# A hybrid transformer stack in FP32: value projections by 512 columns, and five pieces of the engines' queues in another order

## The chip, the cores and the metric

The kernel runs on one core of one Trainium2 chip. The metric is the device time of one execution in microseconds (us), the median of several. TensorE (PE) multiplies, and its weight loads (PEld) run beside the multiplications; VectorE (DVE), ScalarE (ACT) and GpSimd (POOL) do the elementwise work; SyncE (SP) issues the DMAs. Each engine works through its own queue in order, and the queues meet at semaphores.

## The reference

Two blocks of two layers each run over 512 tokens of width 1024, all in FP32. Block one, per layer: feed-forward, a mixer (stick-breaking attention beside a gated delta rule), cross attention to a memory of 256 tokens, feed-forward. Block two, per layer: forgetting attention beside dilated attention (eight heads each), then a gated embedding. What the change touches:

```python
# block one, delta rule: its output is normed and gated before the output projection
go = gated_delta_rule(gq, gk, gv, g, beta)        # solves (lower + eye) per chunk of 64
go = rms_norm(go, gdn_out_norm) * silu(gdn_z)
# block one, memory: keys and values of 256 tokens, 1024 columns each
k, v = split(rms_norm(mem, mem_norm) @ w_kv, 2)
# block two: 512 tokens; values of 512 columns for each kind of head
z = rms_norm(h, norm_g) @ w_in                    # qa ka va ga fa qb kb vb gb
qa, ka, qb, kb = (rms_norm(heads) for each); qb, kb = partial_rope(qb), partial_rope(kb)
oa = forgetting_attention(qa, ka, va, log_f) * silu(ga)
ob = dilated_attention(qb, kb, vb) * silu(gb)
h = h + concat([oa, ob]) @ w_out
```

## The kernel before

**Slabs.** All weights lie in one stream of slabs, a slab being 128 partitions by 2048 numbers (1 MB): the 1024 rows of 256 columns of a weight matrix, as eight chunks of 128 rows. SP loads slab g into one of three buffers `slab_raw` as soon as slab g-3 is used up. ACT copies it, rounded, to `slab_hi` (two buffers, `high`, L313), and DVE writes the rest to `slab_lo` (`low`, L320). Each product of two FP32 matrices is three matmuls, hi·hi, hi·lo and lo·hi (`products`, L340), into PSUM banks.

**A projection stage** (`Project`) walks its slabs. On PE a slab of kind "pair" is 48 matmuls of 512 moving columns (the tokens), with the weights stationary. A slab of kind "tokens" (`tokens`) turns this round, since values are wanted with tokens on partitions: a block of 128 tokens is stationary and the slab's 256 columns move, so 96 matmuls of 256 columns for 512 tokens, 48 for the memory's 256. DVE's queue per slab: the stage's side work, the evacuation of the slab's banks, then `low` of the slab two further on. ACT's: side work, then `high` of the slab two further on. Four banks (0 to 3) take turns.

**Memory stage** (`cross_memory`): three slabs of keys (s = 0 to 2), four of values (s = 3 to 6), once per layer of block one. Its side work `GdnNorm` norms the delta rule's output: DVE scales (L2401, four operations) and multiplies with the gate (L2406, four) at s = 2, ACT rounds (L2377) at s = 3, DVE takes the rest (L2415) at s = 4.

**Delta rule's inverse** (`Mixer.vector`): the triangular inverse of 16 units (chunks 0 to 3 of four heads) is built by steps. For chunks 2 and 3 DVE prepares masks, units and transposes (`vector_first`, `vector_unit`, `vector_turn`), and PE's second product of the first step waits for the transpose of chunk 3. `vector_queries` (L2258) is an operation of DVE that this chain doesn't need.

**Block two's projection** has 15 slabs (4 query/key, 2 value, 2 gate slabs of the forgetting heads; 4, 2 and 1 of the dilated ones). Its side work `HeadNorm` norms the heads and turns the dilated ones (rope): PE rotates into banks 6 and 7, DVE multiplies with the sine (L1181, reads the banks) and the cosine (L1182) and adds (L1184).

**Attention stage** (`AttendPairs`), once per layer of block two: 24 units, three to each of eight head pairs. Per unit PE computes scores, DVE takes the row maximum (`top`, L2967), ACT the exponential (`exp`, L2923), DVE and POOL divide by the sum (`invert`, L2981; POOL L2900), PE transposes (`turn`, L2843), DVE and ACT copy out of PSUM (`keep`, L2988, L2932/L2933), PE multiplies with the values (`out`, L2860). The last gate slab is multiplied here too (`gate(0)`, `gate(1)`, 24 matmuls each, into banks 6 and 7), between the scores of the first units. POOL also writes the low half of the result of each head pair (`low`, L2910).

## Time and profile before

| | |
|---|---|
| median of 3 runs | 3196.43 us (3195.23 to 3198.82) |
| profiled execution | 3195.29 us, of which the span of the trace 3193.6 us |
| PE busy | 3146.7 us, 99% of the span, 17438 matmuls |
| PEld, DVE, ACT, POOL busy | 82%, 52%, 43%, 6% |
| mean DMA rate | 86 GB/s, 275 MB in all |

The span is the time from the first to the last instruction of the trace. Durations of matmuls overlap (the next begins before the last has ended), so the pace of PE is read from the starts of instructions. `[x <-engine tile line]` at a row's end is the time its engine stood idle ahead of it, and what ended that.

### The profile page before, as it was taken

To read this page: it belongs to the slowest core of one execution; us is meant where nothing else is said; L and a number is where in the kernel's file an instruction comes from. 1 tells how busy PE (TensorE), PEld (TensorE's weight loads), DVE (VectorE), ACT (ScalarE), POOL (GpSimd) and SP (SyncE) were. 2 spreads that over 40 slices of the span, in tenths; PEclk is the share of its full clock that TensorE was granted. 3 is DMA by queue.
4 is the path that set the end of the run, shared out by engine and by line. 5 is a ranking of instruction groups with operands and counts; after the bars stand their busy time and mean duration, and the time that the engine had idled before them with its cause. 6 is when DMAs were issued, how large, how long until landed. Compare 5 with 4: busy or idle time off the path is not lost.

```text
span 3193.6 us, 40800 instructions
## 1 busy us (share of the span) xinstructions
PE 3146.7 (99%) x17438; PEld 2612.5 (82%) x17438; DVE 1658.8 (52%) x2253; ACT 1363.0 (43%) x1759; POOL 188.3 (6%) x222
## 2 busy tenths in 40 slices
PE   9999999999999999999999999999999998999999
PEld 7888887898788888888887788788888886788777
DVE  5443348755544433443347855544433568554674
ACT  5222238554433223222226753432223557454663
POOL 0000001300000000000001300000000005000050
PEclk9999999999999999999999999999999999999999
DMA  4222221122122222222321112122222220122202
GB/s 178 94 88 94 109 72 61 41 106 93 66 92 100 86 100 101 102 93 86 112 80 67 54 67 107 66 92 93 102 89 103 80 93 28 71 104 83 80 29 85
DMA packets 47476, 275.13 MB, mean 86 GB/s; under 512 B 5312, under 2 KB 8896, under 8 KB 22208
## 3 DMA queue, kind: packets, MB, share of 16 engines
q1 hardware_dynamic: 47296, 272.53, 23.6%
q8 instruction: 138, 2.26, 0.3%
q14 instruction: 42, 0.34, 0.0%
HBM read 270.41 MB, written 2.10 MB: 85 GB/s over the span
## 4 chain that ended last, share of the span: by engine, by line
PE 90%; DVE 5%; ACT 3%; issue 1%; POOL 0%; DMA 0%; SPq 0%; DVEq 0%; ACTq 0%; POOLq 0%
PE banks L340 80%; PE banks L1617 1%; PE banks L2546 1%; PE banks L2587 1%; ACT slab_hi L313 1%; ACT weights L2923 1%; DVE weights L2967 1%; PE banks L1775 1%; PE banks L1653 1%; PE banks L1632 1%; PE banks L1252 0%; PE banks L1602 0%; DVE slab_lo L320 0%; DVE weights_turned L2988 0%; PE banks L1788 0%
## 5 line engine op out<-in xcount | busy, mean ns | idle before, releaser
L340 PE MATMUL banks<-x_hi,slab_hi 128*128 128x512 f32 x2560 | 1007.5, 394 | 9.6 <-DVE dil_qk L1182 7.9
L340 PE MATMUL banks<-x_hi,slab_lo 128*128 128x512 f32 x2560 | 998.2, 390 | 0.0
L340 PE MATMUL banks<-x_lo,slab_hi 128*128 128x512 f32 x2560 | 997.8, 390 | 0.0
L313 ACT ACTIVATE slab_hi<-slab_raw 128x2048 fp32r<-128x2048 f32 (+2 forms) x274 | 479.7, 1751 | 912.9 <-PE banks L340 912.9
L320 DVE TENSOR_TENSOR slab_lo<-slab_raw,slab_hi 128x2048 fp32r<-128x2048 f32 (+2 forms) x272 | 568.0, 2088 | 413.9 <-ACT slab_hi L313 413.9
L340 PEld LDWEIGHTS banks<-x_hi,slab_hi 128*128 128x128 f32 x2560 | 481.7, 188 | 116.2 <-issue 14.3
L340 PEld LDWEIGHTS banks<-x_lo,slab_hi 128*128 128x128 f32 x2560 | 481.9, 188 | 101.8 <-issue 2.9
L340 PEld LDWEIGHTS banks<-x_hi,slab_lo 128*128 128x128 f32 x2560 | 481.4, 188 | 101.2
L340 PE MATMUL banks<-hidden_hi,slab_hi 128*128 128x512 f32 x704 | 273.9, 389 | 0.0
L340 PE MATMUL banks<-hidden_lo,slab_hi 128*128 128x512 f32 x704 | 273.9, 389 | 0.0
L340 PE MATMUL banks<-hidden_hi,slab_lo 128*128 128x512 f32 x704 | 273.9, 389 | 0.0
L884 DVE TENSOR_TENSOR hidden<-banks,rstd 128x512 f32<-128x512 f32 x88 | 60.7, 690 | 311.1 <-PE banks L340 311.1
L861 DVE SCALAR_TENSOR_TENSOR h<-banks,h 128x512 f32<-128x512 f32 x80 | 55.2, 690 | 208.7 <-PE banks L340 208.6
L893 ACT ACTIVATE hidden_hi<-hidden 128x512 fp32r<-128x512 f32 x88 | 55.6, 632 | 252.9 <-DVE hidden L901 252.9
L340 PEld LDWEIGHTS banks<-hidden_lo,slab_hi 128*128 128x128 f32 x704 | 132.2, 188 | 27.6
L340 PEld LDWEIGHTS banks<-hidden_hi,slab_hi 128*128 128x128 f32 x704 | 132.2, 188 | 27.4
L340 PEld LDWEIGHTS banks<-hidden_hi,slab_lo 128*128 128x128 f32 x704 | 132.2, 188 | 27.3
L1224 POOL MEMSET token_w<- 128x1024 f32 x4 | 3.8, 954 | 2036.7 <-PE banks L340 2036.7
L340 PE MATMUL banks<-slab_hi,x_hi 128*128 128x256 f32 x384 | 109.0, 284 | 0.0
L340 PE MATMUL banks<-slab_hi,x_lo 128*128 128x256 f32 x384 | 108.6, 283 | 0.0
L340 PE MATMUL banks<-slab_lo,x_hi 128*128 128x256 f32 x384 | 108.6, 283 | 0.0
L890 ACT ACTIVATE silu_gate<-silu_gate 128x512 f32<-128x512 f32 x88 | 55.7, 632 | 117.7 <-DVE silu_gate L884 117.7
(402 smaller groups left out, 4191.6 us busy)
## 6 DMA issues: line engine op xcount, KB each, us to landing
slab_raw<-slabs SPq DMA_DIRECT2D x195, 1024.0 KB, 4.8
slab_raw<-slabs SPq DMA_DIRECT2D x64, 704.0 KB, 3.9
slab_raw<-slabs SPq DMA_DIRECT2D x16, 640.0 KB, 3.8
h<-xT SPq DMA_DIRECT2D x8, 256.0 KB, 5.5
memory<-memT SPq DMA_DIRECT2D x2, 1024.0 KB, 5.7
out<-h SPq DMA_DIRECT2D x7, 256.0 KB, 5.1
constants<-con SPq DMA_DIRECT2D x1, 1412.5 KB, 9.9
slab_raw<-slabs SPq DMA_DIRECT2D x4, 256.0 KB, 4.9
```

Of the source, the lines that this page charges most:

```text
L313: self.nc.scalar.activation(self.wh[:, g % self.HIGHS, 0:w], self.raw[:, g % self.RAWS, 0:w], ACT.Copy).then_inc(self.hi_ready, 1)
L320: self.nc.vector.tensor_tensor(self.wl[:, g % self.RAWS, 0:w], self.raw[:, g % self.RAWS, 0:w], self.wh[:, g % self.HIGHS, 0:w].bitcast(F3 ...
L340: mm = self.nc.tensor.matmul(out, left[a], right[c], start=start and n == 0, stop=stop and n == 2)
L861: k.nc.vector.scalar_tensor_tensor(out=h, in0=k.ps[:, jobs[n].bank, :], scalar=self.scale, in1=h, op0=ALU.mult, op1=ALU.add).then_inc(k.ba ...
L884: k.nc.vector.tensor_tensor(to, k.ps[:, jobs[n].bank, :], k.rstd[:], ALU.mult).then_inc(k.bank_free, 1)
L890: k.nc.scalar.activation(a, a, ACT.Silu).then_inc(k.act_done, 1)
L893: k.nc.scalar.activation(self.hh[:, i, :], self.hid[:, i % 2, :], ACT.Copy).then_inc(k.hh_ready, 1)
L1617: mm = nc.tensor.matmul(sc[:, to:to + n], (self.tail if j == b else self.full)[:], part[:, at:at + n], start=False, stop=True, skip_group_ ...
L1632: mm = nc.tensor.matmul(ps[64 * c:64 * c + 64, 2, b * P:S], v[:, b, (2 * p + c) * SB_DIM:(2 * p + c + 1) * SB_DIM], self.prob[:, at:at + n ...
L1653: nc.tensor.matmul(bank, k.c("heads64") if ITEMS[j][0] == "o" else k.ones[:], sq, start=True, stop=True) \
L1775: mm = nc.tensor.matmul(self.product_bank(g)[rows, u - 8 * g, :], self.lm[n][rows, u, :], self.d[rows, u, :], start=True, stop=True, skip_ ...
L2546: mm = nc.tensor.matmul(self.scores_of(u), self.q[:, 2 * h + c, tb * P:(tb + 1) * P], self.kt[:, 2 * h + c, :], start=c == 0, stop=c == 1)
```

## The change

- Value projections of block two and of the memory become kind "wide": two neighbouring slabs are loaded as two halves by rows, each DMA taking 1024 numbers per partition from both slabs, and a matmul moves 512 columns (256 from each part of the buffer). Half as many matmuls; sums run over both slabs of a pair, so all banks of the pair fill in its second slab, and DVE evacuates them there (`WideOut`). The values of the mixer stay as they were.
- `GdnNorm`: of its parts, the gate product moves from s = 2 to s = 3, ACT's rounding from 3 to 5, the rest from 4 to 6.
- `Mixer.vector`: `vector_unit(2)` goes ahead of `vector_lower(3)`, `vector_queries(2)` behind the first `vector_change`.
- `AttendPairs`: the sine of the last rope goes first, into a buffer of its own, then `top` of two units, then cosine and sum; `gate(0)` waits for the sine alone. The split of the next stage's first slab (`high`, `low`) leaves the end of the projection stage and comes between the first units. `gate(1)` is cut into two halves, one before and one behind the first unit's transposes.
- POOL's `low` of head pair 5 goes behind its last division.

```diff
@@ load @@
-            at, w = self.order[g]
+            at, w, *half = self.order[g]
...
+            if half:
+                to = to.rearrange("p (s w) -> p s w", s=2)
+                of = self.slabs[at:at + 2, :, half[0] * w // 2:(half[0] + 1) * w // 2].rearrange("s p w -> p s w")
@@ Project.scalar, and the same in Project.vector for low @@
-            if s or not self.first:
+            if (s or not self.first) and not (self.split_later and s == len(self.slabs) - 1):
                 self.k.high(act, self.g0 + s + 2)
@@ Project @@
+    def wide(self, pe, r, s, i):
+        k = self.k
+        xh, xl, cols = r.moving
+        jobs, second = self.jobs[s + 1 - i % 2], i % 2
+        for tb, job in enumerate(jobs):
+            if not second and job.n >= k.BANKS:
+                pe.wait_ge(k.bank_free, job.n - k.BANKS + 1)
+            out = k.ps[:, job.bank, :].rearrange("p (s c) -> p s c", s=2)
+            t = slice(tb * P, (tb + 1) * P)
+            for n in range(KC // 2):
+                kk = second * KC // 2 + n
+                mm = k.products(out, (xh[:, kk, t], xl[:, kk, t]), k.wide_weights(self.g0 + s, n),
+                                kk == 0, kk == KC - 1)
+            if second and tb + 1 < len(jobs):
+                mm.then_inc(k.half_done, 1)
+        mm.then_inc(k.slab_used, 1)
@@ WideOut @@
+        to = self.dest[:, n, i // 2 * S:(i // 2 + 1) * S]
+        k.nc.vector.tensor_scalar(to, k.ps[:, jobs[n].bank, :], self.columns[:, n:n + 1], None, ALU.mult) \
+            .then_inc(k.bank_free, 1)
@@ AttendPairs.tensor @@
-        pe.wait_ge(*self.heads.parts.at(8))
-        gate(0)
+        pe.wait_ge(*self.heads.parts.at(7))
+        gate(0, 0, KC)
         score(2)
-        gate(1)
+        gate(1, 0, KC // 2)
         for u in range(units):
             turn(u, 0)
             turn(u, 1)
+            if u == 0:
+                gate(1, KC // 2, KC)
@@ AttendPairs.gpsimd @@
-            if u % self.UNITS == 1 and u >= 2 * self.UNITS:
+            if u % self.UNITS == 1 and 2 * self.UNITS <= u < (HEADS2 - 1) * self.UNITS:
                 self.low(pool, u // self.UNITS - 2)
-        for p in (HEADS2 - 2, HEADS2 - 1):
+        for p in range(HEADS2 - 3, HEADS2):
@@ AttendPairs.scalar @@
         exp(1)
+        k.high(act, self.g0 + 1)
         exp(2)
-        for n in range(2):
-            self.gates.scalar(k, act, self.jobs, n, 1)
+        self.gates.scalar(k, act, self.jobs, 0, 1)
         for u in range(units):
-            if u and u + 2 < units:
+            if u > 1 and u + 2 < units:
                 exp(u + 2)
             keep(u)
+            if u == 0:
+                self.gates.scalar(k, act, self.jobs, 1, 1)
+            elif u == 1:
+                exp(3)
```

DVE's queue at the start of the attention stage of block two's first layer; `head_squares` and `last_sine` hold the sine product, `dil_qk` the dilated queries and keys, the ISA rows are `top`. First as it was:

```order
1477 L829 TENSOR_TENSOR gate<-banks,rstd 128x512 [waits slab_used]
1478 L320 TENSOR_TENSOR slab_lo<-slab_raw,slab_hi 128x2048 [waits slab_hi_ready]
1479 L1181 TENSOR_TENSOR head_squares<-banks,constants 128x1024 [waits headnorm_rotated]
1480 L1182 TENSOR_TENSOR dil_qk<-dil_qk,constants 128x1024
1481 L1184 TENSOR_TENSOR dil_qk<-dil_qk,head_squares 128x1024 [waits headnorm_parts]
1482 L603 SCALAR_TENSOR_TENSOR h<-h,final_gain,h_squares 128x512
1483 L2967 ISA weights,minus_row_max<-banks,causal_wide 128x128 [waits attend_z,headnorm_done]
```

and as it is now:

```order
1473 L859 TENSOR_TENSOR gate<-banks,rstd 128x512 [waits slab_used]
1474 L1223 TENSOR_TENSOR last_sine<-banks,constants 128x1024 [waits headnorm_rotated]
1475 L3031 ISA weights,minus_row_max<-banks,causal_wide 128x128 [waits attend_z]
...
1487 L1233 TENSOR_TENSOR dil_qk<-dil_qk,constants 128x1024
1488 L1235 TENSOR_TENSOR dil_qk<-dil_qk,last_sine 128x1024 [waits headnorm_parts]
1489 L611 SCALAR_TENSOR_TENSOR h<-h,final_gain,h_squares 128x512
1490 L3041 RECIPROCAL row_scale<-row_sum 128x4 [waits attend_exp,headnorm_done]
```

The sine product now stands right behind the last evacuation of the projection, and the slab's split (`slab_lo`) is gone from here; it comes back in two halves of 1024 columns around the first unit's `keep`.

DVE's queue in the memory stage of the first layer, from the norm's scaling (s = 2) to the split that ends s = 3; `xa_k` are the keys, `gdn_normed` the delta rule's output. Before:

```order
396 L2401 SCALAR_TENSOR_TENSOR gdn_normed<-l_transposed,params,gdn_squares 128x512 [waits item_rstd,z_silu]
397 L2401 SCALAR_TENSOR_TENSOR gdn_normed<-l_transposed,params,gdn_squares 128x512 [waits item_rstd] x3
398 L2406 TENSOR_TENSOR gdn_normed<-gdn_normed,gdn_z 128x512 [waits gn_y] x4
399 L829 TENSOR_TENSOR xa_k<-banks,memory_rstd 128x256 [waits half_done]
400 L829 TENSOR_TENSOR xa_k<-banks,memory_rstd 128x256 [waits slab_used]
401 L320 TENSOR_TENSOR slab_lo<-slab_raw,slab_hi 128x2048 [waits slab_hi_ready]
402 L2410 SCALAR_TENSOR_TENSOR sb_out<-sb_out,params,head_squares 128x512 [waits item_rstd]
403 L846 TENSOR_TENSOR xa_v<-banks,memory_rstd_column 128x2x256 [waits slab_used]
404 L320 TENSOR_TENSOR slab_lo<-slab_raw,slab_hi 128x2048 [waits slab_hi_ready]
```

Now:

```order
396 L2457 SCALAR_TENSOR_TENSOR gdn_normed<-l_transposed,params,gdn_squares 128x512 [waits item_rstd,z_silu]
397 L2457 SCALAR_TENSOR_TENSOR gdn_normed<-l_transposed,params,gdn_squares 128x512 [waits item_rstd] x3
398 L859 TENSOR_TENSOR xa_k<-banks,memory_rstd 128x256 [waits half_done]
399 L859 TENSOR_TENSOR xa_k<-banks,memory_rstd 128x256 [waits slab_used]
400 L323 TENSOR_TENSOR slab_lo<-slab_raw,slab_hi 128x2048 [waits slab_hi_ready]
401 L2462 SCALAR_TENSOR_TENSOR sb_out<-sb_out,params,head_squares 128x512 [waits item_rstd]
402 L2466 TENSOR_TENSOR gdn_normed<-gdn_normed,gdn_z 128x512 [waits gn_y] x4
403 L323 TENSOR_TENSOR slab_lo<-slab_raw,slab_hi 128x2048 [waits slab_hi_ready]
```

The gate product (four operations) went behind the split of the slab that PE takes as s = 4, and the first slab of values has no evacuation of its own any more.

## Rows read from the trace of the kernel before

**Rows 1.** The page, part 1: busy time, share of the span, instructions.

```profile
PE 3146.7 (99%) x17438; PEld 2612.5 (82%) x17438; DVE 1658.8 (52%) x2253; ACT 1363.0 (43%) x1759; POOL 188.3 (6%) x222
```

**Rows 2.** Waits of PE: for whom, us in total, times, longest us.

```profile
PE banks L340 <- DVE dil_qk L1182: 7.9, 2, 4.0
PE banks L340 <- DVE slab_lo L320: 3.7, 2, 1.9
```

**Rows 3.** PE's timeline (start us, us, what): slab of keys, slab of values.

```profile
2493.64 0.39 PE L340 MATMUL banks<-x_hi,slab_hi 128*128 128x512 f32 x1
...
2504.55 0.95 PE L1258 MATMUL banks<-constants,token_rows 128*128 128x8 f32 x8
...
2506.37 0.28 PE L340 MATMUL banks<-slab_hi,x_hi 128*128 128x256 f32 x1
...
2517.87 0.40 PE L1162 MATMUL banks<-head_squares_hi,heads_r 128*128 128x512 f32 x1
```

**Rows 4.** PE's timeline, memory stage from s = 4, and the next stage's start.

```profile
688.16 0.38 PE L340 MATMUL banks<-slab_hi,memory_hi 128*128 128x256 f32 x1 [1.86 <-DVE slab_lo L320]
...
706.84 0.40 PE L340 MATMUL banks<-x_hi,slab_hi 128*128 128x512 f32 x1
```

**Rows 5.** Timelines of DVE and ACT in the memory stage.

```profile
682.75 2.50 DVE L2406 TENSOR_TENSOR gdn_normed<-gdn_normed,gdn_z 128x512 f32<-128x512 f32 x4
...
685.82 2.28 DVE L320 TENSOR_TENSOR slab_lo<-slab_raw,slab_hi 128x2048 fp32r<-128x2048 f32 x1
...
681.62 1.90 ACT L313 ACTIVATE slab_hi<-slab_raw 128x2048 fp32r<-128x2048 f32 x1
```

**Rows 6.** PE's timeline, `gate(0)` and what follows it, in both layers.

```profile
2645.21 0.76 PE L340 MATMUL banks<-x_hi,slab_hi 128*128 128x512 f32 x1 [3.97 <-DVE dil_qk L1182]
...
2652.28 0.70 PE L3226 MATMUL banks<-fox_qk 64*128 64x512 f32 x2
...
3011.23 0.77 PE L340 MATMUL banks<-x_hi,slab_hi 128*128 128x512 f32 x1 [3.97 <-DVE dil_qk L1182]
...
3019.52 0.70 PE L3226 MATMUL banks<-fox_qk 64*128 64x512 f32 x2
```

**Rows 7.** Stretches: us, busy us of PE, PEld, DVE, ACT, POOL, PEclk, DMA share, GB/s.

```profile
2645.00:2648.00 3.00, 2.79 (x7) 2.24 (x8) 2.97 (x10) 0.42 (x3) 0.00 (x0) 0.50 0.00 0
...
689.00:692.00 3.00, 3.00 (x17) 3.00 (x16) 3.00 (x3) 2.00 (x4) 0.00 (x0) 0.50 0.50 210
```

**Rows 8.** DVE's timeline ahead of `gate(0)`.

```profile
2640.51 2.29 DVE L320 TENSOR_TENSOR slab_lo<-slab_raw,slab_hi 128x2048 fp32r<-128x2048 f32 x1 [1.32 <-ACT slab_hi L313]
...
2643.85 1.22 DVE L1182 TENSOR_TENSOR dil_qk<-dil_qk,constants 128x1024 f32<-128x1024 f32 x1
```

**Rows 9.** PE's timeline, transposes of units 1 and 2, first layer.

```profile
2661.24 0.59 PE L2843 MATMUL banks<-constants,weights 64*128 64x64 f32 x12 [0.52 <-ACT weights_turned L2933]
...
2665.17 0.71 PE L2843 MATMUL banks<-constants,weights 64*128 64x64 f32 x16 [1.65 <-ACT weights_turned L2933]
```

**Rows 10.** POOL and PE at the end of the attention stage, both layers.

```profile
2714.73 1.44 POOL L2910 TENSOR_TENSOR x_lo<-h_squares,x_hi 128x512 fp32r<-128x512 f32 x1
...
2717.77 0.46 PE L2843 MATMUL banks<-constants,weights 64*128 64x64 f32 x8 [1.03 <-POOL weights L2900]
...
2720.04 0.50 PE L340 MATMUL banks<-x_hi,slab_hi 128*128 128x512 f32 x1
...
3085.02 0.43 PE L2843 MATMUL banks<-constants,weights 64*128 64x64 f32 x4 [1.03 <-POOL weights L2900]
...
3088.69 0.50 PE L340 MATMUL banks<-x_hi,slab_hi 128*128 128x512 f32 x1
```

**Rows 11.** DVE's timeline in the first step of the inverse.

```profile
604.28 0.69 DVE L2258 TENSOR_TENSOR decay<-banks,decay 128x512 f32<-128x512 f32 x1
```

**Rows 12.** DVE's timeline, evacuations in the second slab of dilated values, first layer.

```profile
2626.55 1.28 DVE L846 TENSOR_TENSOR dil_v<-banks,rstd_column 128x512 f32<-128x512 f32 x2
```

**Rows 13.** The page, part 6: DMA issues, KB each, us from issue to landing.

```profile
slab_raw<-slabs SPq DMA_DIRECT2D x195, 1024.0 KB, 4.8
```

101 lines of the change are left out of this document (66 added, 35 removed).

## Prediction

> **What bounds the kernel now.** I read the busy times first: PE is busy for 99% of the span [rows 1], so a microsecond is gained only where PE has fewer or shorter matmuls, where it stands idle, or where it runs at a lower clock. Next come PE's waits: twice 4.0 us for DVE's cosine product at the start of the attention stage, twice 1.9 us for the split of a slab in the memory stage [rows 2], twice 1.0 us for POOL at the end of attention [rows 10]. The change aims at all three, 13.7 us together. Last come the timeline of PE around those waits and the granted clock there. After a wait the same matmul takes longer: in the stretch from 2645 to 2648 the granted clock is 0.50, the lower of its two levels (1.2 instead of 2.4 GHz), and the same from 689 to 692 [rows 7]. Both follow a wait of PE. So a wait costs more than its own length here, and that is the second thing the reader has to see.
>
> **The wide matmuls.** PE's pace is the distance of starts. A slab of keys, 48 matmuls of 512 columns, takes 2504.55 - 2493.64 = 10.91 us, 0.2273 each. A slab of values, 96 of 256 columns, takes 2517.87 - 2506.37 = 11.50 us, 0.1198 each [rows 3]. Two of 256 cost 0.2396, so each wide matmul in their place saves 0.0123 us. Block two has 2 layers x 2 pairs of slabs x 4 token blocks x 8 chunks x 3 = 384 of them, the memory 2 x 2 x 2 x 8 x 3 = 192: 576 x 0.0123 = 7.1 us, all of it on PE's path. The bounds are nothing, if a moving operand in two pieces of 256 pays the fixed part twice, and 7.1; I take 7.1, since the columns streamed are the same and only the number of instructions differs. The Trainium skill (TensorE: Matmul & The Clock Gate, section Back-to-back issue gap) gives a warm matmul its columns at 2.4 GHz and only 2.5 ns on top; by that the 576 would bring 1.4 us. The trace shows 13 to 14 ns on top at either width, and the measurement decides.
>
> A wide pair fills its banks only in its second slab, where DVE has four evacuations. In the first layer's dilated values DVE came to them late already, at 2626.55, held by the rope's operations [rows 12]. The one evacuation pair (1.28 us) of the first slab no longer stands ahead of these, so I put the start at about 2625.3 and the second of the four done at 2626.6, while PE wants its bank about 1.2 us earlier than before, at about 2626.2. Cost 0.5 us, bounds 0 and 1.3. In the second layer and for the forgetting heads DVE is earlier, and I count nothing.
>
> **Memory stage, each of two layers.** PE waits 1.86 us at 688.16 for the split that DVE does at 685.82; ahead of that stands the gate product, 682.75 to 685.2, 2.4 us [rows 4, 5]. With that behind the split, the split starts near 683.5 (ACT's half ends there: 681.62 + 1.90) and ends near 685.8; PE's preceding slab ends at 686.3, or 686.0 when wide. The wait goes: 2 x 1.86 = 3.7 us. What is late next: before PE's next slab boundary, 24 wide matmuls or 5.45 us on, DVE must do the moved gate product and the next split, 2.5 + 2.3 us, and one small operation. That fits, with some 0.3 us left; if it doesn't, some tenths come back. After the wait PE took 706.84 - 688.16 = 18.68 us for 144 matmuls [rows 4] that cost 17.25 at the pace of rows 3. The 1.4 us between are the low clock. Without the wait I count them as gained, 2 x 1.4 = 2.9 us; bounds 0 and 2.9.
>
> **Start of the attention stage, each of two layers.** DVE now does the split (2640.51, 2.29 us, itself 1.3 us after the evacuation because ACT's half is waited for), the sine, and the cosine from 2643.85 [rows 8], and only then PE starts `gate(0)` at 2645.21 after 3.97 us idle [rows 6]. With the split moved and the wait on the sine alone, the sine runs from about 2639.5 to 2640.7, before PE has done the scores of units 0 and 1 (2641.24). The whole wait goes: 2 x 3.97 = 7.9 us. The clock: 24 matmuls cost 5.45 us at full pace, but `gate(0)` took 2652.28 - 2645.21 = 7.07 and 3019.52 - 3011.23 = 8.29 us [rows 6], 1.6 and 2.8 too much: 4.4 us, bounds 0 and 4.4.
>
> What is delayed in return: the exponentials of units 0 and 1 now come early, behind two `top`; the cosine and sum (2.4 us) go behind them, so DVE divides unit 0 near 2646.7, while PE is in `gate(0)` until 2646.7 and in the first half of `gate(1)` until about 2650.7. The split of the next slab, 1.9 us on ACT and 2.3 on DVE in two halves, lies under the two halves of `gate(1)` (2.7 us each), on engines that stood idle for more than that there. Then the units. Before, PE waited 1.65 us at unit 2 for ACT, which had two gate activations and a table load to do before it came to the units [rows 9]. Following DVE, ACT and POOL through the new order I find PE waiting about 0.9 us for POOL at unit 2 and 0.3 at unit 3, instead of 0.52 at unit 1 and 1.65 at unit 2. That is 1.0 us, and 0.2 more since fewer evacuations stand between the units: gain 1.2 us a layer, 2.4 in all; bounds 0 and 2 x 2.2.
>
> **End of the attention stage.** POOL's low half of pair 5 (1.44 us) stood ahead of the last division [rows 10]; behind it, POOL has finished 1.4 us sooner, and PE's wait of 1.03 us goes, 2.1 us in two layers. The low half itself is needed some 7 us into the next stage, which takes its input chunk by chunk. In the second layer the stretch from there to the next stage took 3088.69 - 3085.02 = 3.67 us, in the first 2720.04 - 2717.77 = 2.27 [rows 10]: 1.4 us of low clock, counted as gained, bounds 0 and 1.4.
>
> **Inverse.** `vector_queries` (0.69 us) [rows 11] leaves the chain to the transpose that PE waits for; but two pairs of operations that used to alternate now follow each other directly and wait for each other. Gain 0.4 us, twice: 0.8; bounds 0 and 1.4.
>
> **Sum.** 7.1 - 0.5 + 3.7 + 2.9 + 7.9 + 4.4 + 2.4 + 2.1 + 1.4 + 0.8 = 32.2 us. The profiled execution took 3195.3 us with its span of 3193.6; it becomes 3163.1. The median lies 1.1 us above it: 3164.2 us.
>
> **Rivals.**
> - *The clock does not come back* (0.18). The lower clock may answer to all small waits of PE in a stretch, and some remain, or it falls somewhere new. For: it is at its lower level after 1.86 us of waiting as after 3.97. Against: at unit 2 PE stood for 1.65 us and went on at full pace. Then 2.9 + 4.4 + 1.4 = 8.7 us stay: 3172.9.
> - *The wide matmuls bring little* (0.10). Two pieces pay twice, or the fixed part is not per instruction: 3164.2 + 7.1 = 3171.3. By the rate of the Trainium skill named above it would be 3169.9.
> - *Loads of 4 KB pieces are late in the memory stage* (0.04). The slabs of values now come in pieces of 4 KB instead of 8. A slab now lands in 4.8 us [rows 13], 0.65 us ahead of ACT's need at 5.45 us a slab, and the bytes stay the same. If landing doubled to 9.6 us, load, ACT's half and DVE's (9.6 + 1.9 + 2.3) would have to fit in two slabs: 6.9 us a slab instead of 5.45, 1.45 x 4 x 2 = 11.6, and 2.9 of low clock: 3178.7.
> - *Slower: the moving operand in two pieces streams badly* (0.04). No row shows a matmul of this width whose moving side is in two far parts. It decides from 32.2 / 576 = 0.056 us each on top, a pace of 0.283 instead of 0.2273. At half pace it would cost 576 x 0.227 = 131 us: 3295.
> - *More small waits go* (0.04): those of the units, and of the inverse at its upper bound: 3159 or below.
>
> **How the numbers follow.** The forecast has 0.60 and by itself spans 3159 to 3169. With the rivals of the clock and of the wide matmuls in full, and the bounds of the units' waits, 3156 to 3176 leaves out about a tenth. A measurement of this kernel can tell about 0.2%, 6.4 us, from no change. All cases but the slower one are faster by more than that: faster 0.95, same 0.02 and slower 0.03 (the slower rival's 0.04, a small part of which ends near zero, and a rest).
>
> **What would show it.** Right: no wait of PE for `dil_qk` L1233 or for `slab_lo` in the memory stage; the wide matmuls start every 0.227 us; the granted clock is 1.0 through `gate(0)`; no wait for POOL in the last unit; a short wait on a bank behind the first layer's dilated values. Wrong: a wide pace of 0.24 or more; the clock at 0.5 in other places; waits of ACT on loads in the memory stage; new waits of PE at units 1 to 4 of more than 2 us together.

## The result, and the profile after

| | before | changed |
|---|---|---|
| median | 3197.01 us (4 runs, 3195.23 to 3198.82) | 3170.28 us (4 runs, 3167.02 to 3172.95) |
| profiled execution, its span | 3195.29, 3193.6 us | 3171.46, 3169.7 us |
| PE busy, matmuls | 3146.7 us, 17438 | 3138.1 us, 16862 |

The ratio is 0.9913, with a 95% interval of 0.9901 to 0.9926: 26.7 us faster, where 32.2 were forecast. The same kernel, measured once more beside the experiments, had a median of 3167.08 us (ratio 0.9904, 0.9890 to 0.9918). The eight executions of it lie between 3165.4 and 3173.0 with a median of 3168.3, more than 7 us apart, and that spread is a part of the finding.

Most steps of the forecast can be seen in PE's waits. This is the view of rows 2, of the changed kernel (for whom, us in total, times, longest):

```profile
PE banks L2900 <- ACT weights_turned L2993: 9.1, 18, 0.6
...
PE banks L2900 <- POOL weights L2960: 1.8, 2, 0.9
...
PE banks L348 <- DVE dil_v L888: 0.5, 1, 0.5
```

Both rows of [rows 2] are gone: no wait for `dil_qk`, none for `slab_lo`. The wait on a bank behind the first layer's dilated values is there, and its idle time is as large as forecast. The row for POOL is no longer the end of the attention stage, [rows 10], but unit 2 at its start. PE's timeline at the places of the forecast (start us, us, what, idle before):

```profile
2502.82 0.39 PE L348 MATMUL banks<-slab_hi,x_hi 128*128 128x512 f32 x1
...
2513.71 0.39 PE L1205 MATMUL banks<-head_squares_hi,heads_r 128*128 128x512 f32 x1
...
685.59 0.39 PE L348 MATMUL banks<-slab_hi,memory_hi 128*128 128x512 f32 x1
...
707.98 0.39 PE L348 MATMUL banks<-x_hi,slab_hi 128*128 128x512 f32 x1
...
2635.92 0.50 PE L348 MATMUL banks<-x_hi,slab_hi 128*128 128x512 f32 x1
...
2641.59 0.70 PE L3298 MATMUL banks<-fox_qk 64*128 64x512 f32 x2
...
2653.73 0.46 PE L2900 MATMUL banks<-constants,weights 64*128 64x64 f32 x8 [0.88 <-POOL weights L2960]
...
2656.69 0.59 PE L2900 MATMUL banks<-constants,weights 64*128 64x64 f32 x12 [0.55 <-ACT weights_turned L2993]
...
2705.50 0.71 PE L2900 MATMUL banks<-constants,weights 64*128 64x64 f32 x16 [0.25 <-ACT weights_turned L2993]
...
2708.02 0.50 PE L348 MATMUL banks<-x_hi,slab_hi 128*128 128x512 f32 x1
```

- Block two's wide slab: 48 matmuls in 2513.71 - 2502.82 = 10.89 us, 0.2269 each, the pace of keys in [rows 3].
- The memory's wide slabs: 96 in 707.98 - 685.59 = 22.39 us, without a wait, but at 0.2333 each.
- `gate(0)` starts with no wait and takes 2641.59 - 2635.92 = 5.67 us, against 7.07 and 8.29 in [rows 6].
- The last unit no longer waits for POOL; from its transposes at 2705.50 to the next stage it is 2.52 us, where before 2716.28 to 2720.04 was 3.76 (the first of these starts with the last unit's first half).

What was not forecast is the granted clock. The same view as [rows 7], in the mixer, where the change does next to nothing, and at the start of attention:

```profile
608.00:618.00 10.00, 10.00 (x204) 10.00 (x202) 3.98 (x7) 4.65 (x7) 7.98 (x7) 0.53 0.02 3
636.00:641.00 5.00, 5.00 (x24) 5.00 (x24) 1.77 (x3) 0.60 (x1) 0.00 (x0) 0.50 0.00 0
1829.00:1832.00 3.00, 3.00 (x63) 3.00 (x62) 1.45 (x3) 0.60 (x1) 3.00 (x3) 0.51 0.03 5
2636.00:2642.00 6.00, 6.00 (x26) 4.64 (x28) 5.55 (x15) 4.86 (x13) 1.28 (x2) 1.00 0.23 96
2993.00:2999.00 6.00, 6.00 (x28) 4.52 (x28) 4.98 (x14) 4.74 (x13) 1.65 (x2) 1.00 0.22 90
```

The column to read is the third from the end. At `gate(0)` the clock is 1.00 in both layers, as hoped. In the first layer's mixer it stands at 0.50 for ten microseconds and then for more than five again, longer than anywhere in the kernel before, whose mixer shows this:

```profile
607.00:611.00 4.00, 4.00 (x88) 4.00 (x89) 0.83 (x2) 1.05 (x2) 4.00 (x4) 0.57 0.02 6
1853.00:1856.00 3.00, 3.00 (x17) 2.88 (x16) 1.17 (x2) 0.00 (x0) 0.00 (x0) 0.50 0.00 0
```

**Where the time went, stage by stage.** ACT starts to round every slab once its buffer is free, in every kernel in the same sequence, so the starts of one slab's rounding in two profiles tell how far they have drifted apart. For instance the slabs behind the first layer's mixer and behind its memory stage, before:

```profile
659.64 1.91 ACT L313 ACTIVATE slab_hi<-slab_raw 128x2048 fp32r<-128x2048 f32 x1
...
701.42 1.92 ACT L313 ACTIVATE slab_hi<-slab_raw 128x2048 fp32r<-128x2048 f32 x1 [3.76 <-PE banks L340]
```

and changed:

```profile
664.76 1.91 ACT L316 ACTIVATE slab_hi<-slab_raw 128x2048 fp32r<-128x2048 f32 x1
...
697.04 1.92 ACT L316 ACTIVATE slab_hi<-slab_raw 128x2048 fp32r<-128x2048 f32 x1 [1.59 <-DMA slab_raw<-slabs]
...
702.64 1.92 ACT L316 ACTIVATE slab_hi<-slab_raw 128x2048 fp32r<-128x2048 f32 x1 [1.60 <-PE banks L348]
```

So the changed kernel enters the memory stage 5.12 us later than before, and leaves it only 1.22 later: the stage is 3.90 us shorter. (The line at 697.04 shows ACT waiting for a load of the new kind, 1.59 us. PE had work until then, so it costs nothing. A wait of ACT on such a load was one of the prediction's signs of being wrong; it stands here once, without the cost.) Done for the stages that differ, in us against the profile of before; the labels are those of the experiments, and "fox values" are the value slabs of the forgetting heads:

| | mixer 1 | memory 1 | mixer 2 | memory 2 | fox values, 2 layers | attention 1 | attention 2 |
|---|---|---|---|---|---|---|---|
| changed | +5.90 | -3.90 | -0.66 | -3.89 | -2.57 | -7.20 | -10.49 |
| after_again | -0.03 | -3.90 | +1.18 | -3.89 | -2.57 | -7.22 | -10.54 |
| only_wide | +0.58 | -0.14 | +2.68 | -1.67 | -2.57 | +1.13 | -2.19 |
| only_attention | +0.56 | -0.01 | 0.00 | -1.52 | 0.00 | -6.79 | -9.39 |
| only_norm | +0.14 | -3.59 | +2.62 | -3.58 | 0.00 | +1.55 | -0.02 |
| only_inverse | -0.10 | -0.02 | -0.13 | 0.00 | 0.00 | +0.10 | +0.07 |
| filled_thin | -1.06 | -3.90 | -1.68 | -3.89 | -2.57 | -7.21 | -10.54 |
| wait_back | +0.48 | -3.90 | -1.67 | -3.88 | -2.58 | -4.35 | -6.13 |

("attention" includes the dilated values just ahead of it.) Outside the mixer the changed kernel's two profiles agree to 0.1 us: 28.1 us less than before. The mixer gives 5.24 of it back in the first profile and 1.15 in the second. One difference stands in no column: ahead of the first mixer the two profiles are already 0.78 and 0.58 us ahead of before, from the first ten microseconds of the execution, which the change doesn't touch; there the profiles of the table differ by up to 2 us.

### The profile page after: what moved, and what is told of

It is laid out like the page before. It is cut to its first block, busy times and chain, and to the rows that moved or that the text cites. A ratio compares the mean times of both kernels' runs of the same rounds, so it can differ in the third digit from the quotient of the medians.

```text
span 3169.7 us, 39642 instructions
## 1 busy us (share of the span) xinstructions
PE 3138.1 (99%) x16862; PEld 2581.1 (81%) x16862; DVE 1660.8 (52%) x2255; ACT 1362.5 (43%) x1759; POOL 190.5 (6%) x222
## 4 chain that ended last, share of the span: by engine, by line
PE 92%; DVE 4%; ACT 2%; issue 1%; DMA 0%; POOL 0%; DVEq 0%; SPq 0%; ACTq 0%; POOLq 0%
PE banks L348 81%; PE banks L1673 1%; PE banks L2602 1%; PE banks L2643 1%; ACT weights L2983 1%; PE banks L1831 1%; DVE weights L3031 1%; PE banks L1709 1%; PE banks L1688 1%; PE banks L1308 0%; PE banks L1658 0%; PE banks L1844 0%; DVE weights_turned L3052 0%; PE banks L3298 0%; PE banks L466 0%
## 5 line engine op out<-in xcount | busy, mean ns | idle before, releaser
L2960 POOL TENSOR_SCALAR weights<-weights,row_scale 128x128 f32<-128x128 f32 (+1 forms) x64 | 80.2, 1258 | 417.2 <-DVE row_scale L3041 417.2
L945 DVE TENSOR_TENSOR hidden_lo<-hidden,hidden_hi 128x512 fp32r<-128x512 f32 x88 | 61.0, 693 | 61.5 <-ACT hidden_hi L935 61.5
L417 ACT ACTIVATE x_hi<-h,params 128x512 fp32r<-128x512 f32 x72 | 50.9, 712 | 88.6 <-DVE h L903 68.9
```

Of the source, the lines that this page charges most:

```text
L417: k.nc.scalar.activation(self.x[0][:, c, :], k.h[:, c, :], ACT.Copy, scale=self.gain[:, c:c + 1]) \
L945: k.nc.vector.tensor_tensor(self.hl[:, i, :], hid, self.hh[:, i, :].bitcast(F32), ALU.subtract) \
L2960: ins = self.k.nc.gpsimd.tensor_scalar(w, w, self.col(self.ri, tb, 1), None, ALU.mult)
```

## The experiments

The kernel before beside them had medians of 3197.8, 3198.2 and 3197.6 us in the three groups of four.

### The parts, one by one

**only_wide.** From the change, only this and what it calls:

```diff
-                           Run(4, self.at("xa_v"), SLAB, y, TokensOut(self.xv, k.mcol), "tokens")],
+                           Run(4, self.at("xa_v"), SLAB, y, WideOut(self.xv, k.mcol), "wide")],
-            Run(2, self.at(f"{n}_v"), SLAB, moving, TokensOut(v, k.rcol), "tokens"),
+            Run(2, self.at(f"{n}_v"), SLAB, moving, WideOut(v, k.rcol), "wide"),
```

> The kernel before with the wide values alone (block two and memory), everything else as it was. Three prices for the 576 wide matmuls, less 0.5 us for the wait on a bank. A, the prediction's: 0.0123 us each, 7.1 - 0.5 = 6.6 us faster. B, by the paces that the changed kernel's trace shows: 384 in block two at 0.2269 us against 2 x 0.1198, and 192 in the memory stage at 0.2333 against 2 x 0.1183: 4.9 + 0.6 - 0.5 = 5.0 us faster. C, two far pieces pay their fixed part twice: nothing gained. By the Trainium skill's 2.5 ns on top of a warm matmul (TensorE: Matmul & The Clock Gate, section Back-to-back issue gap) it would be 1.4 - 0.5 = 0.9 us. The wait of 1.86 us in the memory stage and the low clock behind it should stay as they were.

Measured: 3194.37 us (11 runs, 3188.6 to 3200.7), ratio 0.9988, 0.9980 to 0.9997: 1.0 to 6.4 us faster. Price B, 5.0, lies well within, A (6.6) just outside, C and the 0.9 just outside below. The times are wide; the stages are not: 2.57 us for the two layers' forgetting values (192 wide matmuls, 0.0134 each, a little above the 0.0123 forecast), and 0.14 us in the first memory stage for 96. (That first stage keeps its wait of 1.86 us and the low clock behind it. The cleaner figure is the changed kernel's 3.90 against 3.59 in only_norm: 0.31 us for the 96. The other entries of its line are low clock: a stretch less in the second memory stage, where PE's wait of 1.86 us is still there, and one more in the first attention stage and in the second mixer.)

**only_attention.** The changes to `AttendPairs`, `HeadNorm` and the split of the next slab:

```diff
-        pe.wait_ge(*self.heads.parts.at(8))
-        gate(0)
+        pe.wait_ge(*self.heads.parts.at(7))
+        gate(0, 0, KC)
         score(2)
-        gate(1)
+        gate(1, 0, KC // 2)
```

> The kernel before with the changes to the attention stage alone: its start, first units and end, and the rope's own buffer. Waits that go: 7.9 at the start, 2.1 at the end, 0.9 in the units; the second cut of the gate product costs 0.5: 10.4 us. Theory A: the low clock behind these waits goes with them, 1.4 + 2.6 + 1.4 us by the durations of the gate product and the last stretch: 15.8 us faster. Theory B: the same amount of low clock falls somewhere else in the kernel: 10.4 us faster, and the profile shows new stretches at a granted clock of 0.50 outside the attention stage, or longer ones. The prediction's own terms would give 18.2.

Measured: 3180.28 us (5 runs, 3177.6 to 3181.8), ratio 0.9947, 0.9934 to 0.9959: 13.1 to 21.1 us faster. A (15.8) is in, B (10.4) is out. The stages give 6.79 + 9.39 = 16.2. The clock at the stage's start and where the mixer had been low:

```profile
632.00:635.00 3.00, 3.00 (x16) 3.00 (x16) 1.60 (x3) 0.00 (x0) 0.00 (x0) 0.53 0.00 0
...
2640.00:2646.00 6.00, 6.00 (x30) 4.57 (x28) 5.55 (x13) 4.59 (x13) 1.56 (x2) 1.00 0.18 74
```

The low clock at attention went with its wait, and did not come back at another place to the same amount. The mixer has its short one, somewhere else than before (632 instead of 607).

**only_norm.** The three steps of `GdnNorm` at s = 3, 5 and 6 instead of 2, 3 and 4.

```diff
-        elif s == 4:
+        elif s == 6:
             for c in range(4):
                 dve.wait_ge(*self.hi_ready.at(c + 1))
```

> The kernel before with only the delta rule's output norm queued later (the gate product behind the split, the rounding and the rest two slabs later); the values of the memory stay at 256 columns. The wait of 1.86 us goes in both layers: 3.7 us. Theory A: the low clock behind it (two stretches of 3.4 us at half clock, 1.7 us each) goes too: 3.7 + 3.4 = 7.1 us faster. Theory B: it falls elsewhere: 3.7 us faster, with low clock at a new place in the profile.

Measured: 3190.76 us (11 runs, 3187.4 to 3195.4), ratio 0.9981, 0.9972 to 0.9990: 3.2 to 9.0 us faster, which holds both. The stages decide it: 3.59 and 3.58 us shorter, the wait of 1.86 and 1.7 of low clock in each; from 689 to 692 the clock is 1.00, where [rows 7] has 0.50. But the same profile has ten microseconds of low clock in the second mixer, which take back 2.6:

```profile
1849.00:1859.00 10.00, 9.32 (x60) 9.01 (x59) 2.58 (x5) 1.19 (x2) 0.00 (x0) 0.54 0.00 0
...
689.00:692.00 3.00, 3.00 (x28) 3.00 (x27) 3.00 (x5) 2.79 (x5) 0.00 (x0) 1.00 0.80 333
```

**only_inverse.** DVE's queue in the first step of the inverse.

```diff
         self.vector_first(dve, 2)
+        self.vector_unit(dve, 2)
         self.vector_lower(dve, 3)
-        self.vector_queries(dve, 2)
-        self.vector_unit(dve, 2)
```

> The kernel before with only the order of DVE's queue in the first step of the inverse changed. The prediction's term: 0.8 us faster. By the changed kernel's trace the idle time ahead of the product goes from 0.97 to 0.89 us, so 0.2 us in both layers. Rival: the new order is what draws the long stretches of low clock into the mixer that the changed kernel shows (10.2 us at half clock behind the first step of the first layer, 6.8 near its last step, against 3.4 before): then this kernel shows them as well and is 3 to 7 us slower than before. If they are absent here, the order is not their cause.

Measured: 3196.93 us (11 runs, 3192.6 to 3200.9), ratio 0.9997, 0.9988 to 1.0006. The mixers are 0.10 and 0.13 us shorter. The rival has fallen: with the new order alone the mixer's low clock is as short as before, and only_norm and only_wide have the long one with the old order.

The four medians are 3.4, 17.5, 7.0 and 0.8 us below that of before, 28.7 together; the whole change gives 26.7 and 31.1 in its two measurements. Within the spread of the times, no part is seen to help or hinder another.

### The clock in the mixer

**after_again.** No edit.

> The changed kernel once more, with no edit, so that its low clock is seen in a second execution and its time in more of them. In the first profile three stretches at half clock cost 10.2 us of PE's time, all in the mixer: 608 to 618, 635 to 642 and 1829 to 1832. Theory A: they hang on the kernel's own sequence; then they stand at the same places again and the time is again 3171. Theory B: the mixer's many small matmuls and short waits only make it possible, and whether a stretch falls there, and how long it is, differs from execution to execution: then the places or lengths differ, the single times spread over some 6 us (3165 to 3172, as the four known ones do), and a profile with less of it is shorter by half the low time that it lacks.

Measured: 3167.08 us (4 runs, 3165.4 to 3169.8). The profiled execution has a span of 3165.8 us, 3.9 less than the first, and another clock:

```profile
607.00:611.00 4.00, 4.00 (x95) 4.00 (x91) 1.07 (x3) 1.91 (x3) 4.00 (x4) 0.62 0.02 4
612.00:618.00 6.00, 5.60 (x176) 5.41 (x178) 5.22 (x10) 3.23 (x8) 4.13 (x4) 1.00 0.01 3
636.00:641.00 5.00, 4.38 (x40) 4.19 (x39) 3.30 (x7) 1.79 (x3) 0.00 (x0) 1.00 0.00 0
1823.00:1832.00 9.00, 8.92 (x168) 8.95 (x169) 4.55 (x8) 3.07 (x4) 8.88 (x8) 0.50 0.01 2
```

From 612 to 618 the very same instructions now run at 1.00 that had 0.50 before, and the second layer has the long stretch instead. Theory B: the kernel's mixer makes low clock possible, and how much of it an execution gets differs. The mean granted clock of each execution agrees: of the eight, the three fastest (3165.4 to 3167.0 us) have 0.999, the two slowest (3171.5 and 3173.0) 0.996. The kernel before varies in the same way: its 27 executions beside the first four experiments lie between 3194.5 and 3201.8 us, with mean clocks from 0.996 down to 0.993.

**after_filled.** PE's waits in the inverse are filled with matmuls that nothing needs; the part shown is the heart of it.

```diff
+    def fill(self, pe, bank, n):
+        for i in range(n):
+            self.k.nc.tensor.matmul(self.k.ps[:, bank, 0:P], self.k.c("ident"), self.k.c("cumul", 0, P), start=True,
+                                    stop=True, skip_group_check=True)
@@ tensor_change, n == 0, g == 0 @@
+                pe.wait_ge(*self.vb_kept.at(3))
+                self.fill(pe, 5, 6)
         pe.wait_ge(*self.m1_copied.at(self.step(n, g)))
@@ tensor_product, n == 0, g == 1 @@
+                self.fill(pe, 5, 7)
@@ tensor_product, n > 0 @@
+            self.fill(pe, 4 + g, 2)
             pe.wait_ge(*self.d_ready.at(TB + 2 * (n - 1) + g + 1))
```

> The changed kernel with matmuls of 128 columns that nothing needs, put into PE's waits in the delta rule's inverse: 6 ahead of the first change, 7 ahead of the product that waits 0.9 us, 2 ahead of each later product that waits 0.3 us. Their results go to a bank that is overwritten. At 0.115 us each they just fill the waits. If the low clock in the mixer answers to PE's pauses there, the stretches at 0.50 go from the inverse and the time falls by up to 10 us against this profile of the changed kernel, by some 5 against its median. If it answers to the kind of work (products of 64 by 64), the stretches stay, and the time is the same or up to 2 us longer, where the filling outlasts a wait.

Measured: 3179.35 us (5 runs, 3174.6 to 3180.2), 11 us longer than the changed kernel. The expectation had the price wrong. The profile shows why:

```profile
604.62 1.61 PE L1840 MATMUL banks<-constants 128*128 128x128 f32 x12
...
607.21 1.83 PE L1840 MATMUL banks<-constants 128*128 128x128 f32 x14
```

Six matmuls of plain FP32 are twelve passes: from 604.62 to the next instruction at 606.15 it is 1.53 us, 0.255 each, twice what I had taken from rows that count passes. So more was put in than fits. That is one half of the price. Measured as in the table above, the two mixers take 14.5 us longer than filled_thin's, the next experiment; two stretches of 6.8 us at half clock account for 6.8 of these, and 7.7 are left for the overfilling. The clock was 1.00 through all of the filled part and fell behind it in both layers, where waits had been left alone:

```profile
603.00:634.00 31.00, 30.47 (x731) 28.56 (x730) 20.99 (x39) 14.09 (x30) 14.53 (x14) 1.00 0.12 37
637.00:643.00 6.00, 6.00 (x36) 5.88 (x36) 1.76 (x3) 0.60 (x1) 0.00 (x0) 0.54 0.00 0
1859.00:1865.00 6.00, 5.32 (x37) 5.01 (x36) 1.56 (x3) 0.59 (x1) 0.00 (x0) 0.54 0.00 0
```

**filled_thin.** Fewer of them, and the last change as well.

```diff
-                self.fill(pe, 5, 6)
+                self.fill(pe, 5, 3)
-                self.fill(pe, 5, 7)
+                self.fill(pe, 5, 3)
-            self.fill(pe, 4 + g, 2)
+            if g == 1 or n == 1:
+                self.fill(pe, 4 + g, 1)
@@ tensor_last_product, tensor_last_change @@
+        if g == 1:
+            self.fill(pe, 5, 1)
...
+        if g == 1:
+            self.fill(pe, 7, 2)
```

> The changed kernel with PE's waits in the inverse filled by fewer matmuls that nothing needs: 3 ahead of the first change, 3 ahead of the product that waits 0.9 us, 1 ahead of each product that waits 0.3 us, and 2 ahead of the last change (0.68 us), which the first filling left out. One costs 0.255 us (six took 1.53 us in the first filling, two passes each), so 14 of them, 3.6 us a layer, lie within waits of 4.3 us. Theory A: the low clock in the mixer answers to PE's pauses there; then the time is shorter than the changed kernel's by what low clock its profiles show (6.8 to 10.2 us), less what falls behind the inverse, where a wait of 0.6 us stays: 3160 to 3165. Theory B: it answers to the small products; then no gain, 3167 to 3170, and the stretches at 0.50 stand in the inverse as before.

Measured: 3164.26 us (4 runs, 3163.8 to 3166.6), ratio 0.9893, 0.9874 to 0.9913: 4.0 us below the median of the changed kernel's eight runs, within what theory A gave. The interval of the ratio overlaps that of the changed kernel (0.9890 to 0.9918), so the times alone don't prove the gain. The profile is clearer: the mixers are 1.06 and 1.68 us shorter than before (table above), where the changed kernel's four lie between 0.66 shorter and 5.90 longer. Both mixers at full clock, in one row each:

```profile
603.00:641.00 38.00, 37.15 (x802) 34.93 (x803) 26.82 (x50) 16.42 (x33) 13.97 (x13) 1.00 0.09 28
1818.00:1857.00 39.00, 37.62 (x805) 35.26 (x804) 27.62 (x51) 17.22 (x36) 14.70 (x15) 1.00 0.10 29
```

Of the 22 mixers in the eleven profiles without filling (with that of before, the changed kernel's two, and all other experiments), 20 have a stretch at 0.50; of the four in filled_thin and thin_aligned, none. That low clock in the mixer answers to PE's pauses rather than to the small products is thereby well supported. That a pause is all there is to it is not shown: the filling also adds larger matmuls.

**wait_back.** The reverse: a wait is put back at the start of attention.

```diff
-        pe.wait_ge(*self.heads.parts.at(7))
+        pe.wait_ge(*self.heads.parts.at(8))
```

> The changed kernel with one edit: the gate product at the start of the attention stage waits for the cosine product again, as before the change, and not for the sine alone. The cosine now ends at 2638.6 in the profile and PE is done with the scores at 2636.0, so PE waits 2.7 us in each layer, 5.3 us together. Theory A: such a wait brings a stretch at half clock with it. Then the granted clock is 0.50 right behind it in both layers, at 1.4 to 2.6 us each, and the kernel is 8 to 10 us slower than the changed one, less what the units' waits for POOL (0.88) give back. Theory B: the low clock at this place came from something else that the change took away (the split beside it, the order of the units); then 3.5 to 5.3 us slower, with the clock at 1.00 there.

Measured: 3173.84 us (5 runs, 3172.5 to 3179.7), 5.5 us above the changed kernel's median, in two groups: three runs near 3173 and two near 3179.5. The profile:

```profile
2632.59 0.47 PE L348 MATMUL banks<-x_hi,slab_hi 128*128 128x512 f32 x1 [2.76 <-DVE dil_qk L1233]
...
2992.29 0.47 PE L348 MATMUL banks<-x_hi,slab_hi 128*128 128x512 f32 x1 [2.76 <-DVE dil_qk L1233]
```

```profile
2633.00:2636.00 3.00, 3.00 (x15) 2.45 (x14) 2.12 (x5) 1.69 (x1) 1.44 (x2) 1.00 0.00 0
2995.00:2997.00 2.00, 2.00 (x6) 1.52 (x6) 0.00 (x0) 0.00 (x0) 0.36 (x1) 0.52 0.00 0
```

The wait is the forecast one, twice. In the first layer the clock stays at 1.00 behind it and the stage is 2.86 us longer than filled_thin's; in the second it falls, and the stage is 4.41 longer, 2.76 of wait and 1.65 of clock. So the wait brings the low clock sometimes, and neither theory is right as it stood: A in one layer, B in the other. Nothing is given back by the units.

### The other terms

**after_queues.** Two edits of DVE's and ACT's queues.

```diff
-        self.vector_unit(dve, 2)
         self.vector_lower(dve, 3)
-        self.vector_turn(dve, 2)
-        self.vector_first(dve, 3)
+        self.vector_unit(dve, 2)
+        self.vector_first(dve, 3)
+        self.vector_turn(dve, 2)
@@ AttendPairs.vector, u == 0 @@
+                invert(2)
                 k.low_half(dve, self.g0 + 1, 1)
@@ AttendPairs.scalar @@
-            if u > 1 and u + 2 < units:
+            if u > 2 and u + 2 < units:
                 exp(u + 2)
             keep(u)
+            if u == 2:
+                exp(4)
```

> The changed kernel with two further edits of queues, at places that don't touch. (1) Inverse: the unit of chunk 2 goes back behind the products of chunk 3, so that no operation directly follows the one it needs; the product of keys and queries stays behind the first change. In the changed kernel PE waits 0.89 us there, since a dependent pair takes 0.72 us where an interleaved one takes 0.35. Expected: the wait falls to 0.3 to 0.4 us, in both layers, 1.0 us in all. If the reorder was right and the chain is bound elsewhere, it stays at 0.9. (2) Attention: DVE divides unit 2 right behind the first copy, where it stood idle, and ACT copies unit 2 before the exponential of unit 4. PE's wait for POOL at unit 2, 0.88 us, goes; rival: it comes back at unit 3, where POOL and ACT are bound by the table load of 1.28 us and the exponentials of unit 3; then the two waits together (0.88 + 0.55) fall by 0.4 only. In all 1 to 3 us faster than the changed kernel, which the times can hardly tell and the waits can.

Measured: 3169.46 us (4 runs, 3168.4 to 3172.8), the changed kernel's time. Neither edit gained anything. PE:

```profile
606.45 1.15 PE L1831 MATMUL banks<-inverse,l_masked 64*64 64x64 f32 x32 [0.86 <-issue]
...
2653.49 0.80 PE L2900 MATMUL banks<-constants,weights 64*128 64x64 f32 x12 [1.42 <-DVE weights_turned L3054]
```

At unit 2 the wait is gone, and at unit 3 it is 1.42, which is 0.88 + 0.55 to within a hundredth: the rival, without even the 0.4 I had left it. In the inverse the wait fell by 0.03 instead of 0.5. DVE there, in this kernel:

```profile
604.26 0.95 DVE L2319 TENSOR_TENSOR half_inverse_t<-l_transposed,constants 128x256 f32<-128x256 f32 x1
```

and POOL beside it, in this kernel:

```profile
603.96 0.96 POOL L1590 TENSOR_TENSOR l_masked<-l_transposed,constants 128x256 f32<-128x256 f32 x1 [1.40 <-DVE l_transposed L2308]
```

In the kernel before, POOL's masking ran from 604.33 to 605.06, beside `vector_queries` [rows 11], and the same L2319 (there L2263) took 0.41 us afterwards. Take the 0.69 us operation out from between, and the 0.41 us operation lands beside POOL's and takes 0.95, or 0.69 in the changed kernel. First before, then changed:

```profile
605.26 0.41 DVE L2263 TENSOR_TENSOR half_inverse_t<-l_transposed,constants 128x256 f32<-128x256 f32 x1
```

```profile
604.33 0.69 DVE L2319 TENSOR_TENSOR half_inverse_t<-l_transposed,constants 128x256 f32<-128x256 f32 x1
```

The Trainium skill (SBUF — State Buffer, section "SBUF: two separate sides") has a rule for this: a DVE operation with two inputs in SBUF and a POOL operation that reads SBUF exclude each other for a whole instruction. `vector_queries` reads a bank and escapes it, L2319 reads SBUF twice. The trace agrees. Beside POOL's masking, L2319 ends 0.28 or 0.29 us behind POOL in both kernels, whenever it had started: 605.21 behind 604.92 here, 605.02 behind 604.74 in the changed kernel. And it goes both ways: POOL's operation takes 0.96 us here and 0.73 in the other two, and here it started while DVE was in another operation with two inputs in SBUF (L2325, 603.91 to 604.34).

**aligned.** All tensors of mixer and cross attention 128 bytes further up.

```diff
-        return self.at(name, shape, self.region + offset, dt)
+        return self.at(name, shape, self.region + offset + (128 if offset >= 33000 and name not in ('hidden_lo', 'silu_gate', 'hidden', 'memory_squares', 'memory_in') else 0), dt)
```

(The names left out are the feed-forward's and the memory's input, which stay where they were.)

> The changed kernel with the tensors of mixer and cross attention (memory's split, its keys and values, the queries and the attention's result) 128 bytes further up in memory, nothing else. The wide matmuls of the memory stage start every 0.2333 us, those of block two every 0.2269; the output projection of cross attention, which is not wide, also takes 0.2333. Theory A: it is the place of the other operand (memory's split, the attention's result, both at the same odd offset) that costs 0.0065 us a matmul; then both paces fall to 0.227 and the kernel gains 1.3 us in the memory stage and 2.5 in the output projection. Theory B: it belongs to the stage's traffic or the operands' shape: the paces stay at 0.2333.

Measured: 3166.49 us (4 runs, 3163.3 to 3170.5), ratio 0.9906, 0.9890 to 0.9921, which can't tell 4 us from none. The paces can. First and one past the last of the memory's wide matmuls and of the output projection of cross attention:

```profile
680.40 0.40 PE L348 MATMUL banks<-slab_hi,memory_hi 128*128 128x512 f32 x1
...
702.24 0.39 PE L348 MATMUL banks<-x_hi,slab_hi 128*128 128x512 f32 x1
...
820.89 0.80 PE L348 MATMUL banks<-xa_y_hi,slab_hi 128*128 128x512 f32 x1
...
864.84 0.39 PE L348 MATMUL banks<-x_hi,slab_hi 128*128 128x512 f32 x1
```

96 in 21.84 us is 0.2275, and 192 in 43.95 is 0.2289; in after_again the same took 22.39 (0.2332) and 865.94 - 820.92 = 45.02 (0.2345). Theory A: it is the place in memory, 0.55 and 1.07 us a layer.

**thin_aligned.** The last two together.

> The thin filling together with the tensors of mixer and cross attention 128 bytes further up. The shift took the wide matmuls of the memory stage from 0.2333 to 0.2275 us and those of cross attention's output from 0.2345 to 0.2289: 0.56 and 1.08 us a layer, 3.3 us in all. With theory A of the filling 3157 to 3162, with theory B 3164 to 3167.

Measured: 3161.91 us (4 runs, 3161.6 to 3162.1), ratio 0.9884, 0.9868 to 0.9900: 35.7 us below before, 6.4 below the changed kernel's median, and the fastest version here. The medians of the two fillings differ by 2.4 us where 3.3 were expected. This profile has a stretch of low clock in the first 12 us of the execution (granted clock 0.63 from 9 to 12, against 1.00 in filled_thin); counted from there to the last slab the two differ by 3.4.

Its four runs lie within 0.4 us, but that the spread goes with the mixer's low clock is not shown: those of filled_thin lie within 2.9 us, and those of after_uncut, which has low clock in both mixers, within 0.3.

**after_uncut.** The second gate product in one piece.

```diff
-        gate(1, 0, KC // 2)
+        gate(1, 0, KC)
         for u in range(units):
             turn(u, 0)
             turn(u, 1)
-            if u == 0:
-                gate(1, KC // 2, KC)
```

> The changed kernel with the second gate product in one piece ahead of the first unit, instead of in two halves around its transposes. The cut itself costs PE 0.23 us a layer (the two halves took 2.97 + 2.95 us from start to start, the whole 5.69 before the change). If the cut pays, PE now waits longer at units 1 and 2: before the change 0.52 and 1.65 us stood there, against 0.88 and 0.55 at units 2 and 3 now, so 0.5 to 1 us a layer slower, 1 to 2 in all, seen in the waits rather than in the times. If the early start of the exponentials is what took the waits away and not the cut, the waits stay below 1.4 us and the kernel is up to 0.5 us faster.

Measured: 3171.44 us (4 runs, 3171.4 to 3171.6). PE's waits for ACT, POOL and DVE in all units are 7.4 + 1.9 + 2.2 = 11.5 us against 9.1 + 1.8 = 10.9, so 0.6 more, from which the saved cuts take 0.5: nothing, between the two expectations. What the cut does is to break the pauses up; without it two follow each other,

```profile
2649.86 0.46 PE L2900 MATMUL banks<-constants,weights 64*128 64x64 f32 x8 [1.12 <-DVE weights L3043]
2651.29 0.46 PE L2900 MATMUL banks<-constants,weights 64*128 64x64 f32 x8 [0.96 <-POOL weights L2958]
```

and in this profile low clock stood behind them in both layers: the first attention stage is 5.54 us shorter than before and not 7.20. One profile does not show that this is the rule, though all four runs have the same mean clock, 0.996, and agree to 0.3 us. So how much the low clock differs between executions may itself depend on the kernel; that was not tried further.

## Why the prediction was right, and where not

The time lies in the range, 6 us above the forecast in the first measurement and 3 in the second. The sum has to be taken apart against the profiles. At the last slab they are 23.8 and 27.8 us ahead of before, where 32.2 were forecast. Of the 8.4 us that are missing in the first, 5.2 are low clock in the mixer: the first rival in its second form, "or it falls somewhere new". Of the 4.4 missing in the second, only 1.2 are that. The terms below cost 4.0 in either, and 0.8 and 0.6 us were gained at the start of the execution, by no term. The forecast's own clock terms were right.

- **Wide matmuls, 7.1.** Right in mechanism and in block two: 4 pairs at 1.28 us, 5.1 where 4.7 were in the sum. The slower rival (pieces stream badly) and "two pieces pay twice" have fallen. In the memory stage the term was mis-sized. I gave 192 matmuls the saving of block two, 2.4 us; at 256 columns the memory stage runs at 0.1184 (113 starts from 693.34 to 706.72), at 512 at 0.2333, so 0.0035 x 192 = 0.7, and the stages say 0.31 us a layer. The price belonged to a row of that stage. The 0.0058 that a wide matmul loses there is the place of its operand (aligned).
- **Bank, -0.5.** Right in mechanism and place: 0.45 us idle in the first layer, none in the second. From start to start it costs more:

```profile
2621.22 0.39 PE L1215 MATMUL banks<-to_turn_lo,rope_r 128*128 128x512 f32 x1
2622.06 0.47 PE L348 MATMUL banks<-x_hi,slab_hi 128*128 128x512 f32 x1 [0.45 <-DVE dil_v L888]
2622.37 0.39 PE L348 MATMUL banks<-x_lo,slab_hi 128*128 128x512 f32 x1
```

The two distances are 0.84 + 0.31 = 1.15 us, where two at full pace are 0.45: the wait costs 0.7. The idle column leaves out that matmuls overlap while PE is fed.
- **Memory, 3.7 + 2.9.** Right: 3.59 us a layer in only_norm, 1.86 of it wait and 1.7 clock, so 3.4 for 2.9. The clock was priced against the pace of block two; at the stage's own 0.1184 its 144 matmuls cost 17.05 us and not 17.25, which leaves 1.6 for the clock in place of 1.4. In the sum for this stage that error partly offsets the one in the wide matmuls.
- **Start of attention, 7.9 + 4.4.** The wait is gone whole. `gate(0)` got 1.40 and 2.62 us shorter, 4.0: I had counted against 24 x 0.2273 = 5.45, but even at full clock it is 5.67 to the next instruction.
- **Units, 2.4.** The failed step. The forecast of waits was 0.9 for POOL at unit 2 (0.88) and 0.3 at unit 3 (0.55), and one more of 0.55 at unit 5 where there had been 0.26. And the cut of `gate(1)` itself costs: its halves take 2.97 + 2.95 us from start to start, where before the whole took 5.69 (2653.57 to the transposes at 2659.26). The waits of the first layer's units, without POOL's at the end, went from 5.89 to 5.44 us. Gain 0.45 - 0.23, twice, is 0.4 where I had 2.4. after_queues shows that removing the wait for POOL alone only moves it to unit 3.
- **End, 2.1 + 1.4.** Right. The wait for POOL and the low clock are gone in both layers, at most a few tenths more.
- **Inverse, 0.8.** Mis-sized: 0.23 in only_inverse. The 0.69 us operation did leave the chain, but it had been beside POOL's masking, and what took its place is held up by it. after_queues shows this, and that the order of the rest does not matter.

By these the sum is 5.1 + 0.7 - 0.7 + 3.7 + 3.4 + 7.9 + 4.0 + 0.4 + 2.1 + 1.4 + 0.2 = 28.2 us. Without the 0.2 of the inverse, which lies in the mixer, it is 28.0, and the stages outside the mixer measure 28.1. The terms cost 4.0 of the 32.2.

- **The mixer's clock** is the rest. No term of mine spoke of it, since the change hardly touches the mixer. In the first profile the two mixers took 5.2 us longer than before, in the second 1.2; before and after_again differ by 27.8 us at the last slab, before and the first by 23.8. No one part of the change brings it: only_wide and only_norm, which share no edit, show the same long stretch, in their second mixers, and only_inverse, the one edit of the mixer itself, does not. Whether the kernel before ever has the long stretch, its single profile doesn't show. Low clock, short or long, is there in 20 of 22 mixers, and in the changed kernel's two profiles it differs in place and length. Filled, it is gone, and the kernel then takes 3164.3 us.

The chance that I gave the clock rival, 0.18, was argued from one row, unit 2's wait of 1.65 us with no low clock behind it [rows 9]. That row showed only that such a pause need not bring low clock; wait_back shows both outcomes behind the same 2.76 us, in its two layers. A single profile then says little about how much low clock a kernel has, and a sum made against one profile inherits that profile's share.

## What to carry to other kernels

- Where PE stands idle shortly and often, don't take the low clock of one profile for the kernel's own: take a second profile before the differences between two are explained, and compare stages by a mark that both kernels share instead of whole times. Here single times were more than 7 us apart, and the stages outside the mixer agreed within 0.1.
- A few matmuls that nothing needs, sized to fit inside waits that can't be removed, were worth 4 us by the medians. Price one from a row of its own first: here each plain FP32 matmul was two passes in the profile, and the first filling paid 7.7 us for what didn't fit.
- An operation taken off a chain leaves a hole in time, and what moves into it meets what used to run beside it. Look at the other engines' rows there before the duration is carried over. And a wait that is removed between units of a pipeline is gained only if the next unit's chain has slack.

## What the runs showed of the hardware that was not expected

- Low clock behind pauses much shorter than the Trainium skill would have one avoid (TensorE: Matmul & The Clock Gate, section "Why this matters for your kernels" warns of idle gaps): the longest in the inverse is 0.89 us, and ten microseconds near 0.50 followed it, in the row from 608 to 618. By that rule alone such pauses would be harmless; the trace disagrees.
- 128 bytes of address are worth some 2.4% of a matmul's pace in these two stages: 0.2332 to 0.2275 us with memory's split as the stationary side, 0.2345 to 0.2289 with the attention's result as the moving one. Which alignment it is that counts was not tried.
- Changing from the 512-column matmuls of a gate product to the small transposes and back costs PE 0.2 us, at full clock and without a wait: the two halves of `gate(1)` take 2.97 + 2.95 us, the whole took 5.69.
